# Stick-breaking attention: the mask as a product on TensorE instead of an operation on GpSimd and one on VectorE

## The chip, the cores and the metric

The kernel runs on one NeuronCore of a Trainium2 chip. The metric is the device time of one execution in microseconds (us), lower is better; where several runs are given it is their median. TensorE multiplies matrices into eight PSUM banks, VectorE, ScalarE and GpSimd work element by element, and SyncE issues the transfers of the weights.

## The reference, cut to what matters

The whole program is two stacked blocks of two layers each. The change is in the first block, in both of its layers: 256 tokens, 1024 columns, three attention branches beside each other, gates, an output projection and a feed-forward part. One of the three branches is stick-breaking attention, with 8 heads of 64 columns:

```python
z = jnp.einsum('bqhd,bkhd->bhqk', q_blk, k).astype(jnp.float32) * scale
past = kpos[None, :] < qpos[:, None]
log_beta = jax.nn.log_sigmoid(z)
log_one_minus = jnp.where(past, jax.nn.log_sigmoid(-z), 0.0)
remain = lax.cumsum(log_one_minus, axis=3, reverse=True) - log_one_minus
w = jnp.where(past, jnp.exp(log_beta + remain), 0.0)
return jnp.einsum('bhqk,bkhd->bqhd', w.astype(v.dtype), v)
```

A key counts only where it stands strictly before the query (`past`). The second block holds other mixers and a mixture of experts; it is the longer part of the time and isn't touched.

## The kernel before, in words

All large products are made in three parts: each float32 operand is split into a high part in float32r and a low remainder, and `three` (lines 324 to 330) multiplies high by high, low by high and high by low. Weights come in chunks of 128 x 2048 into a ring of six. For each chunk ScalarE makes the high part (`split`, line 530), VectorE the remainder (`split`, line 642), and TensorE frees the slot. Each engine runs one list of instructions in the order of the code; between engines semaphores count. A PSUM bank is taken with a wait on `free` (`Tensor.bank`) and freed by whoever reads it last.

The program is written by hand in stages, and the stage of the change is `stick_beside_inputs`. There are four routines that carry it, one for each engine, and in all of them stick-breaking attention is woven into the products that make the inputs of the next two branches (jobs QA0, QA1, KVA, QC0, QC1, KC0, KC1, and the values VC).

TensorE (lines 1010 to 1060) goes: logits of heads 0 to 3 into banks 0 to 3; the products of QA0, QA1 and KVA; the sums of heads 0 to 3; QC0; a transposition of values; output of heads 0 and 1; logits of heads 4 and 5; QC1; output of heads 2 and 3; logits of heads 6 and 7; KC0 and KC1; the sums of heads 4 to 7; the first half of VC; output of heads 4 and 5; the second half of VC; output of heads 6 and 7. Logits are keys by queries in three blocks of 128 columns: keys 0 to 127 by all 256 queries (line 1018) and keys 128 to 255 by the later queries (line 1019). Blocks 0 and 2 are the diagonal ones, in which the mask matters. A head has 64 columns, and two heads share a tile of 128 partitions: an even head lies in partitions 0 to 63, an odd one in 64 to 127, so the logits of a head use half of the array's rows.

For a head the chain is: logits; ScalarE takes the magnitude, Exp and Ln in place (lines 1213, 1218, 1223); VectorE adds the positive part (line 1428), which gives the softplus of the logits; GpSimd multiplies the diagonal blocks by 0 or 1 (`stick_heads`, line 843); TensorE adds the sums over later keys to the logits in the bank, by three float32 products (`sums`, lines 1026 to 1028); VectorE adds 0 or -1e30 to the result and writes it to SBUF, and frees the bank (`log_weights`, line 1434); ScalarE takes Exp (line 1228); TensorE multiplies by the values (`weigh_pair`, lines 477 and 478).

VectorE has, beside that and the splits, the turning of queries and keys by position (`turned_by_positions`, lines 712 to 717), called `rope` in the routine: one operation that reads the job's bank, four that read it by quarters of the partitions (line 714, the last of which frees the bank) and one addition. The bank of KC0 is 7, that of QC1 is 6, and VC takes banks 6 and 7.

In the second block, `decays_in` (lines 1778 to 1787) puts two products of 4 rows (256 and 128 columns) and two products of the identity with a mask of 128 columns, in float32, into one bank per head; `latent_heads` (line 1727) has products of 64 rows behind ordinary ones; `key_rows` (lines 1834 and 1835) has products of two heads in both halves of the rows.

Of the kernel before, what the change touches and what calls it, by code (L numbers as in the profile page):

```python
# [24 lines left out]
F32R = mybir.dt.float32r  # L25
# [108 lines left out]
def table_columns(parts):  # L134
# [8 lines left out]
A_TABLES, A_COLS = table_columns(SHARED_TABLES + [  # L143
    ("band", S), ("causal", S), ("before01", 3 * P), ("before", 3 * P), ("tri", P), ("ones", P)])
B_TABLES, B_COLS = table_columns(SHARED_TABLES + [
# [15 lines left out]
class Memory:  # L161


    def __init__(self, nc, ctx):
# [3 lines left out]
        def sem(name):  # L168
            return ctx.enter_context(nc.semaphore(name))
# [20 lines left out]
        self.unit_rows = nc.dram_tensor("unit_rows", (UNITS * P, D), F32, kind="Internal").ap()  # L190
        self.zeros = sb("zeros", [P, P], F32R)
        self.bank = [ctx.enter_context(nc.psum_tensor(f"bank{i}", [P, 512], F32))[:] for i in range(8)]

# [9 lines left out]
        self.x_loaded = sem("x_loaded")  # L203
        self.tables_loaded = sem("tables_loaded")
        self.cols_loaded = sem("cols_loaded")
        self.shared_loaded = sem("shared_loaded")
# [63 lines left out]
        self.n_ready = sem("n_ready")  # L270
        self.lom_ready = sem("lom_ready")
        self.logw_ready = sem("logw_ready")
        self.gate_in = sem("gate_in")
# [522 lines left out]
class Pool(Engine):  # L796
# [40 lines left out]

    def stick_heads(self, before):
        m = self.m
        for h in range(8):  # L840
            a = m.probs[:, h % 4, :].rearrange("p (n c) -> p n c", n=3)[:, 0:3:2, :]
            self.eng.wait_ge(m.n_ready, self.w.next(m.n_ready))
            self.isa.tensor_tensor(a, a, before, ALU.mult).then_inc(m.lom_ready, 1)


# [30 lines left out]
class TensorA(Tensor):  # L876
    def layer(self, layer):
# [9 lines left out]
        for job in STICK_IN[2:]:  # L887
            self.inputs(job)
        self.eng.wait_ge(m.qk_ready, w.next(m.qk_ready, 4))
        self.stick_beside_inputs()  # L890

# [118 lines left out]
    def stick_beside_inputs(self):  # L1010
# [4 lines left out]
        def logits(h):  # L1015
            q, k = (a_tile(m, x + h // 2)[(h % 2) * DH:(h % 2 + 1) * DH, :] for x in (QB, KB))
            bank = self.bank(h % 4)
            self.isa.matmul(bank[:, 0:S], k[:, 0:P], q, start=True, stop=False, skip_group_check=True)
            self.isa.matmul(bank[:, S:S + P], k[:, P:S], q[:, P:S], start=False, stop=False,
                            skip_group_check=True).then_inc(m.to_act[h % 4], 1)  # L1020

        def sums(h):
            bank, lom = m.bank[h % 4], m.probs[:, h % 4, :]
            tri, ones = m.tab(A_TABLES, "tri"), m.tab(A_TABLES, "ones")
            self.eng.wait_ge(m.lom_ready, self.w.next(m.lom_ready))
            self.isa.matmul(bank[:, 0:S], tri, lom[:, 0:S], start=False, stop=False, skip_group_check=True)
            self.isa.matmul(bank[:, P:S], ones, lom[:, S:S + P], start=False, stop=False, skip_group_check=True)
            self.isa.matmul(bank[:, S:S + P], tri, lom[:, S:S + P], start=False, stop=True,
                            skip_group_check=True).then_inc(m.to_dve[h % 4], 1)

# [25 lines left out]
        for half in range(2):  # L1056
            self.used(self.rows(banks, self.chunk(), 512, (m.hT_hi, m.hT_lo), 4, 4 * half, KT))
            if half == 0:
                out(4)
        out(6, 3)  # L1060

# [81 lines left out]
class ScalarA(Scalar):  # L1143
# [62 lines left out]
    def stick_beside_inputs(self, tile0):  # L1206
# [18 lines left out]
        def weights(h):  # L1225
            self.eng.wait_ge(m.logw_ready, self.w.next(m.logw_ready))
            self.eng.wait_ge(m.weighed, self.w.reuse(m.weighed))
            self.isa.activation(m.probsT[:, h % 2, :], m.probs[:, h % 4, :], ACT.Exp).then_inc(m.pt_ready, 1)

# [28 lines left out]
        for h in range(4, 8):  # L1258
            weights(h)
        self.oT_high(5, tile0, (4, 3))  # L1260
        self.inputs_out(VC)
        self.oT_high(7, tile0, (4, 3))

# [57 lines left out]
class VectorA(Vector):  # L1321
# [90 lines left out]
    def stick_beside_inputs(self, tile0, cos, sin):  # L1412
        m = self.m
        neg = m.tab(A_TABLES, "before")

# [14 lines left out]

        def log_weights():
            for hh in range(4):
                self.eng.wait_ge(m.to_dve[hh], self.w.next(m.to_dve[hh]))
                self.isa.tensor_tensor(m.probs[:, hh, :], m.bank[hh][:, 0:384], neg, ALU.add) \
                    .then_inc(m.logw_ready, 1)
                self.eng.drain().then_inc(m.free[hh], 1)

        self.settle()
# [5 lines left out]
        self.split(1)  # L1444
        log_weights()
        rope(QA1)
# [8 lines left out]
        magnitudes()  # L1455
        self.split(1)
        rope(KC0)
        self.split(1)
        log_weights()
        self.split(1)  # L1460
        rope(KC1)
        self.oT_low(2, tile0, (4, 3))
        self.oT_low(3, tile0, (4, 3))

# [1398 lines left out]
def program(nc, inp, out):  # L2863
    with ExitStack() as ctx:
# [52 lines left out]
        def _(pool):  # L2917
# [10 lines left out]
            for layer in range(DEPTH):  # L2928
                e.power((2, 4), 4)
                e.stick_heads(m.tab(A_TABLES, "before01").rearrange("p (n c) -> p n c", n=3)[:, 0:3:2, :])  # L2930

# [115 lines left out]
def tables_a():  # L3047
# [8 lines left out]
        band=np.concatenate([window, causal], 1), causal=np.concatenate([0 * one, causal], 1),  # L3056
        before01=np.concatenate([before, one, before], 1),
        before=np.concatenate([np.where(before, 0.0, NEG), 0 * one, np.where(before, 0.0, NEG)], 1),
        tri=np.where(i[:, None] >= i[None, :], -1.0, 0.0), ones=-one)
# [184 lines left out]
```

## Time and profile before

| | |
|---|---|
| median of 3 runs | 2347.61 us (2345.21 to 2348.76) |
| span of the profiled execution, first to last instruction | 2343.6 us |
| what lies around the span, if the span is that of the median run | 4.0 us |
| TensorE busy | 2297.0 us (98%) |
| VectorE busy | 1882.2 us (80%) |
| ScalarE busy | 1404.5 us (60%) |
| GpSimd busy | 69.3 us (3%) |

The profile is of one execution and gives its span; its device time is not listed apart from the three runs. Names in it: PE is TensorE, PEld its loading of weights, DVE VectorE, ACT ScalarE, POOL GpSimd, SP SyncE. A line such as L1018 is a line of the kernel before; a helper's line stands for all its callers. Products overlap in the pipeline, so the duration of one says less than the distance from one start to the next; the text reads starts. A float32 product leaves two records, one of float32r a single one; the type at the end of a row of TensorE is that of the bank. The stick-breaking stage of layer 0 lies at about 50 to 118 us, that of layer 1 at about 491 to 559 us.

### The profile page before, as it was taken

The page shows a single profiled execution, that of the slowest core. Times are in us where ns is not written, and L with a number is a line of the kernel's source. Part 1 is how long each engine was busy: PE and PEld are TensorE (multiplying, and loading weights), DVE is VectorE, ACT ScalarE, POOL GpSimd, SP SyncE. Part 2 cuts the span into 40 slices and gives each one's busy share as a digit, 9 for nine tenths or more (in the row PEclk, how much of TensorE's full clock was granted, in tenths as well). Part 3 has the DMA queues.
Part 4 walks back from the last instruction along what each step waited for, and adds up shares of the span by engine and source line. Part 5 has one row for each costly group of instructions (what it writes and reads, how often), then busy time and mean ns, then how long its engine had stood idle before and what let it go on. Part 6 is the DMA issues. An engine that isn't in the chain of part 4 may idle for free.

```text
span 2343.6 us, 34973 instructions
## 1 busy us (share of the span) xinstructions
PE 2297.0 (98%) x12998; PEld 1975.8 (84%) x12998; DVE 1882.2 (80%) x2158; ACT 1404.5 (60%) x1396; POOL 69.3 (3%) x81
## 2 busy tenths in 40 slices
PE   9999999999999999989999989999999999999997
PEld 8877999997789998779989778888888888888886
DVE  5977898768779987774457879888988898989897
ACT  5565544455654435634336547777777777777764
POOL 0100000000000000000000010000000000000000
PEclk9999999999999999999999999999999999999999
DMA  6444555444365556268544359999999999999995
GB/s 257 144 162 177 209 190 180 175 168 153 137 219 195 195 181 213 98 224 263 195 179 162 138 230 392 379 376 380 387 376 382 376 385 374 386 374 387 374 398 211
DMA packets 93418, 608.15 MB, mean 259 GB/s; under 512 B 9696, under 2 KB 18032, under 8 KB 22656
## 3 DMA queue, kind: packets, MB, share of 16 engines
q1 hardware_dynamic: 88064, 584.69, 66.3%
q0 software_dynamic: 5248, 22.02, 2.4%
q8 instruction: 70, 1.15, 0.2%
q14 instruction: 36, 0.29, 0.0%
HBM read 591.47 MB, written 15.20 MB: 259 GB/s over the span
## 4 chain that ended last, share of the span: by engine, by line
PE 85%; DVE 8%; DVEq 2%; ACT 2%; issue 1%; DMA 1%; POOL 1%; ACTq 0%; POOLq 0%; SPq 0%
PE bank L328 27%; PE bank L330 26%; PE bank L329 26%; DVEq L634 2%; DVE w_lo L642 2%; DMA raw<-in_weights_dram 1%; PE bank L1978 1%; DVE nat L714 1%; DVE probs L729 1%; PE bank L437 0%; PE bank L447 0%; PE bank L400 0%; PE bank L380 0%; PE bank L477 0%; ACT w_hi L530 0%
## 5 line engine op out<-in xcount | busy, mean ns | idle before, releaser
L642 DVE TENSOR_TENSOR w_lo<-raw,w_hi 128x2048 fp32r<-128x2048 f32 x547 | 1239.1, 2289 | 253.2 <-ACT w_hi L530 230.5
L530 ACT CAST w_hi<-raw 128x2048 fp32r<-128x2048 f32 x547 | 1037.3, 1913 | 223.0 <-DMA raw<-in_weights_dram 215.4
L328 PE MATMUL bank<-w_hi,hT_hi 128*128 128x512 f32 (+1 forms) x1248 | 496.5, 398 | 7.6 <-DVEq L2726 2.6
L330 PE MATMUL bank<-w_hi,hT_lo 128*128 128x512 f32 (+1 forms) x1248 | 486.5, 390 | 0.0
L329 PE MATMUL bank<-w_lo,hT_hi 128*128 128x512 f32 (+1 forms) x1248 | 485.5, 389 | 0.0
L328 PE MATMUL bank<-hT_hi,w_hi 128*128 128x256 f32 x1552 | 443.6, 286 | 2.5 <-DVEq L663 1.7
L330 PE MATMUL bank<-hT_hi,w_lo 128*128 128x256 f32 x1552 | 440.3, 284 | 0.0
L329 PE MATMUL bank<-hT_lo,w_hi 128*128 128x256 f32 x1552 | 440.2, 284 | 0.0
L328 PE MATMUL bank<-w_hi,oT_hi 128*128 128x512 f32 x940 | 370.6, 394 | 1.5 <-DVE oT_lo L2739 1.2
L329 PE MATMUL bank<-w_lo,oT_hi 128*128 128x512 f32 x940 | 366.4, 390 | 0.0
L330 PE MATMUL bank<-w_hi,oT_lo 128*128 128x512 f32 x940 | 366.2, 390 | 0.0
L328 PEld LDWEIGHTS bank<-hT_hi,w_hi 128*128 128x128 f32 x1552 | 298.0, 192 | 6.9 <-issue 4.7
L329 PEld LDWEIGHTS bank<-hT_lo,w_hi 128*128 128x128 f32 x1552 | 298.0, 192 | 1.7 <-issue 0.5
L330 PEld LDWEIGHTS bank<-hT_hi,w_lo 128*128 128x128 f32 x1552 | 297.9, 192 | 0.0
L328 PEld LDWEIGHTS bank<-w_hi,hT_hi 128*128 128x128 f32 x1248 | 235.5, 189 | 60.1 <-issue 13.8
L330 PEld LDWEIGHTS bank<-w_hi,hT_lo 128*128 128x128 f32 x1248 | 235.1, 188 | 49.1
L329 PEld LDWEIGHTS bank<-w_lo,hT_hi 128*128 128x128 f32 x1248 | 235.7, 189 | 44.4
L328 PEld LDWEIGHTS bank<-w_hi,oT_hi 128*128 128x128 f32 x940 | 176.6, 188 | 40.0 <-issue 3.7
L330 PEld LDWEIGHTS bank<-w_hi,oT_lo 128*128 128x128 f32 x940 | 176.4, 188 | 37.5
L329 PEld LDWEIGHTS bank<-w_lo,oT_hi 128*128 128x128 f32 x940 | 176.8, 188 | 34.1
L1549 DVE SCALAR_TENSOR_TENSOR probs<-probs,all_cols 128x254 f32<-128x254 f32 (+1 forms) x176 | 77.3, 480 | 6.9 <-issue 0.4
L1295 ACT ACTIVATE probs<-probs 128x512 f32<-128x512 f32 x22 | 13.9, 633 | 107.0 <-DVE probs L1549 107.0
(314 smaller groups left out, 1586.6 us busy)
## 6 DMA issues: line engine op xcount, KB each, us to landing
raw<-in_weights_dram SPq DMA_DIRECT2D x547, 1024.0 KB, 4.9
token_rows<-all_cols SPq DMA_DIRECT2D x11, 512.0 KB, 9.4
arena<-in_norms_dram POOLq DMA_DIRECT2D x4, 1024.0 KB, 9.2
nat<-token_rows POOLq DMA_DIRECT2D x7, 512.0 KB, 8.1
unit_rows<-probs POOLq DMA_DIRECT2D x7, 512.0 KB, 6.9
arena<-in_b_gate_dram POOLq DMA_DIRECT2D x6, 512.0 KB, 4.1
unit_rows<-all_cols SPq DMA_DIRECT2D x5, 512.0 KB, 9.6
tables<-in_tables_b_dram POOLq DMA_DIRECT2D x1, 1216.0 KB, 5.7
```

The lines of the kernel that those rows point to most:

```text
L328: mm(out, st[0], mv[0], start=start, stop=False, skip_group_check=True)
L329: mm(out, st[0], mv[1], start=False, stop=False, skip_group_check=True)
L330: return mm(out, st[1], mv[0], start=False, stop=stop, skip_group_check=True)
L530: self.isa.copy(m.w_hi[:, slot, :], m.raw[:, slot, :]).then_inc(m.hi_ready, 1)
L634: self.eng.drain()
L642: self.isa.tensor_tensor(m.w_lo[:, slot, :], m.raw[:, slot, :], m.w_hi[:, slot, :].bitcast(F32), ALU.subtract).then_inc(m.lo_ready, 1)
L714: last = self.isa.tensor_tensor(tmp[to:to + 32], src[a:a + 32], s[a:a + 32], ALU.mult)
L729: last = self.isa.tensor_tensor_reduce(m.probs[:, hh, a:e], m.bank[b][:, a:e], mk, self.scale, first(h), ALU.add, ALU.max, m.small[:, 16 + ...
L1295: self.isa.activation(g, g, ACT.Silu).then_inc(m.silu_done, 1)
L1549: last = self.isa.scalar_tensor_tensor(out, bank[:, g * S:(g + 1) * S - back], col(g, 2 - back), out, ALU.mult, ALU.add)
L1978: last = self.isa.transpose(bank[:, k * P:(k + 1) * P], h_rows(m)[:, k * P:(k + 1) * P], m.tab(B_TABLES, "ident"))
```

## The change

GpSimd's mask and VectorE's additions are taken out (with the semaphores `lom_ready` and `logw_ready`), and the two mask tables of 384 columns become one of 128, `hidden`, with 0 or -2^100. A new tile `exact` holds the identity and `hidden` in float32r; GpSimd copies them there once, in layer 0, and TensorE waits for that (`exact_ready`) ahead of the first logits. Behind the two products of every head's logits TensorE gets a third, of the full array: the identity by `hidden`, repeated over blocks 0 and 2, added in the bank. With it the softplus of a hidden logit is zero without a mask, and so is the Exp of its sum. The sums now wait for VectorE's `n_ready` and signal ScalarE, which takes Exp straight from the bank and frees the bank. VectorE's turning of KC0 moves ahead of a split. The output of heads 6 and 7 goes to bank 2 in place of bank 3.

```diff
         def logits(h):
             q, k = (a_tile(m, x + h // 2)[(h % 2) * DH:(h % 2 + 1) * DH, :] for x in (QB, KB))
             bank = self.bank(h % 4)
             self.isa.matmul(bank[:, 0:S], k[:, 0:P], q, start=True, stop=False, skip_group_check=True)
-            self.isa.matmul(bank[:, S:S + P], k[:, P:S], q[:, P:S], start=False, stop=False,
+            self.isa.matmul(bank[:, S:S + P], k[:, P:S], q[:, P:S], start=False, stop=False, skip_group_check=True)
+            later = bank[:, 0:384].rearrange("p (n c) -> p n c", n=3)[:, 0:3:2, :]
+            ident, hidden = m.exact[:, 0:P], m.exact[:, P:2 * P]
+            self.isa.matmul(later, ident, hidden.unsqueeze(1).to_broadcast([P, 2, P]), start=False, stop=False,
                             skip_group_check=True).then_inc(m.to_act[h % 4], 1)
...
         def sums(h):
...
-            self.eng.wait_ge(m.lom_ready, self.w.next(m.lom_ready))
+            self.eng.wait_ge(m.n_ready, self.w.next(m.n_ready))
...
-                            skip_group_check=True).then_inc(m.to_dve[h % 4], 1)
+                            skip_group_check=True).then_inc(m.to_act[h % 4], 1)
...
         def weights(h):
-            self.eng.wait_ge(m.logw_ready, self.w.next(m.logw_ready))
+            self.eng.wait_ge(m.to_act[h % 4], self.w.next(m.to_act[h % 4]))
             self.eng.wait_ge(m.weighed, self.w.reuse(m.weighed))
-            self.isa.activation(m.probsT[:, h % 2, :], m.probs[:, h % 4, :], ACT.Exp).then_inc(m.pt_ready, 1)
+            self.isa.activation(m.probsT[:, h % 2, :], m.bank[h % 4][:, 0:384], ACT.Exp).then_inc(m.pt_ready, 1)
+            self.eng.drain().then_inc(m.free[h % 4], 1)
...
@@ VectorE, stick_beside_inputs
         magnitudes()
         rope(QA0)
         self.split(1)
-        log_weights()
         rope(QA1)
...
         rope(QC1)
         magnitudes()
-        self.split(1)
         rope(KC0)
-        self.split(1)
-        log_weights()
-        self.split(1)
+        self.split(3)
         rope(KC1)
-        self.oT_low(2, tile0, (4, 3))
-        self.oT_low(3, tile0, (4, 3))
+        self.oT_low(2, tile0, (4, 2))
+        self.oT_low(3, tile0, (4, 2))
...
@@ GpSimd, for each layer
                 e.power((2, 4), 4)
-                e.stick_heads(m.tab(A_TABLES, "before01").rearrange("p (n c) -> p n c", n=3)[:, 0:3:2, :])
+                if layer == 0:
+                    pool.wait_ge(m.shared_loaded, 16)
+                    nc.gpsimd.tensor_copy(m.exact[:, 0:P], m.tab(A_TABLES, "ident"))
+                    pool.wait_ge(m.tables_loaded, 16)
+                    nc.gpsimd.tensor_copy(m.exact[:, P:2 * P], m.tab(A_TABLES, "hidden"))
+                    pool.drain().then_inc(m.exact_ready, 1)
```

## Rows read from the trace of the kernel before

**Rows 1.** Page, parts 1 and 4: busy us (share) xinstructions; the chain's shares by engine

```profile
PE 2297.0 (98%) x12998; PEld 1975.8 (84%) x12998; DVE 1882.2 (80%) x2158; ACT 1404.5 (60%) x1396; POOL 69.3 (3%) x81
...
PE 85%; DVE 8%; DVEq 2%; ACT 2%; issue 1%; DMA 1%; POOL 1%; ACTq 0%; POOLq 0%; SPq 0%
```

**Rows 2.** Timeline of TensorE, later sums: start, us, operation, [idle before <- releaser]

```profile
99.90 0.60 PE L1026 MATMUL bank<-probs,tables 128*128 128x256 f32 x2
...
102.12 0.70 PE L1026 MATMUL bank<-probs,tables 128*128 128x256 f32 x2 [0.30 <-POOL probs L843]
...
105.17 0.47 PE L328 MATMUL bank<-w_hi,hT_hi 128*128 128x512 f32 x1 [1.03 <-issue]
...
542.93 0.70 PE L1026 MATMUL bank<-probs,tables 128*128 128x256 f32 x2 [0.68 <-POOL probs L843]
...
545.98 0.47 PE L328 MATMUL bank<-w_hi,hT_hi 128*128 128x512 f32 x1 [1.03 <-issue]
```

**Rows 3.** Timeline of VectorE, layer 0, beside the later sums

```profile
97.26 1.95 DVE L1428 SCALAR_TENSOR_TENSOR probs<-bank,probs 128x384 f32<-128x384 f32 x4
99.13 2.36 DVE L642 TENSOR_TENSOR w_lo<-raw,w_hi 128x2048 fp32r<-128x2048 f32 x1
...
102.28 2.79 DVE L714 TENSOR_TENSOR nat<-bank,tables 32x512 f32<-32x512 f32 x4
```

**Rows 4.** Line 843: operation xcount, ns min/median/max, first and last start

```profile
L843 POOL TENSOR_TENSOR probs<-probs,tables x16: 721/742/2772, 62.3 to 542.8; 128x256 f32<-128x256 f32 x16
```

**Rows 5.** Timelines of GpSimd, ScalarE and TensorE, layer 0, single rows

```profile
22.07 0.72 POOL L835 TENSOR_TENSOR small<-small 128x2 f32<-128x2 f32 x1 [12.36 <-DVE small L682]
...
81.97 0.95 ACT L1228 ACTIVATE probsT<-probs 128x384 f32<-128x384 f32 x2
...
87.43 0.71 PE L1018 MATMUL bank<-arena 64*128 64x256 f32 x4
```

**Rows 6.** Timeline of TensorE, layer 0, logits of heads 0 to 3

```profile
50.44 0.71 PE L1018 MATMUL bank<-arena 64*128 64x256 f32 x4
50.98 0.40 PE L1019 MATMUL bank<-arena 64*128 64x128 f32 x4
...
52.05 0.39 PE L328 MATMUL bank<-hT_hi,w_hi 128*128 128x256 f32 x1
52.27 0.28 PE L329 MATMUL bank<-hT_lo,w_hi 128*128 128x256 f32 x1
52.39 0.29 PE L330 MATMUL bank<-hT_hi,w_lo 128*128 128x256 f32 x1
```

**Rows 7.** Timeline of TensorE, layer 0, logits of heads 4 and 5

```profile
79.81 0.71 PE L1018 MATMUL bank<-arena 64*128 64x256 f32 x4
...
80.67 0.39 PE L328 MATMUL bank<-hT_hi,w_hi 128*128 128x256 f32 x1
80.90 0.28 PE L329 MATMUL bank<-hT_lo,w_hi 128*128 128x256 f32 x1
```

**Rows 8.** Timeline of TensorE, second block, `decays_in`: one head, then the next

```profile
988.88 0.69 PE L1782 MATMUL bank<-nat,tables 4*128 4x256 f32 x2
...
989.73 0.71 PE L1785 MATMUL bank<-tables 128*128 128x128 f32 x4
990.37 0.69 PE L1782 MATMUL bank<-nat,tables 4*128 4x256 f32 x2
```

**Rows 9.** Timeline of TensorE, second block, from an ordinary product to 64 rows

```profile
943.31 0.28 PE L330 MATMUL bank<-hT_hi,w_lo 128*128 128x256 f32 x1
943.52 0.91 PE L1727 MATMUL bank<-arena 64*128 64x128 f32 x8
```

**Rows 10.** Timeline of TensorE, second block, pairs of heads around full-array products

```profile
973.78 0.55 PE L447 MATMUL bank<-tables,probs 128*128 128x128 f32 x3
974.25 0.71 PE L1834 MATMUL bank<-arena 64*128 64x256 f32 x4
```

**Rows 11.** Who waited for whom, TensorE, whole span: us, times, longest

```profile
PE bank L447 <- DVE probs L763: 3.4, 4, 1.2
```

More of the change, by code:

```diff
@@ L143 @@
 A_TABLES, A_COLS = table_columns(SHARED_TABLES + [
-    ("band", S), ("causal", S), ("before01", 3 * P), ("before", 3 * P), ("tri", P), ("ones", P)])
+    ("band", S), ("causal", S), ("hidden", P), ("tri", P), ("ones", P)])
 B_TABLES, B_COLS = table_columns(SHARED_TABLES + [
@@ L191, in __init__ @@
         self.zeros = sb("zeros", [P, P], F32R)
+        self.exact = sb("exact", [P, 2 * P], F32R)
         self.bank = [ctx.enter_context(nc.psum_tensor(f"bank{i}", [P, 512], F32))[:] for i in range(8)]
@@ L204, in __init__ @@
         self.tables_loaded = sem("tables_loaded")
+        self.exact_ready = sem("exact_ready")
         self.cols_loaded = sem("cols_loaded")
@@ L270, in __init__ @@
         self.n_ready = sem("n_ready")
-        self.lom_ready = sem("lom_ready")
-        self.logw_ready = sem("logw_ready")
         self.gate_in = sem("gate_in")
@@ L836, in power @@
             .then_inc(m.rstd, 1)
[L838 to L843, printed above, removed]
 STICK_IN = [
@@ L889, in layer @@
         self.eng.wait_ge(m.qk_ready, w.next(m.qk_ready, 4))
+        if layer == 0:
+            self.eng.wait_ge(m.exact_ready, w.next(m.exact_ready))
         self.stick_beside_inputs()
@@ L1059, in stick_beside_inputs @@
                 out(4)
-        out(6, 3)
+        out(6, 2)
     def turn_values(self):
@@ L1259, in stick_beside_inputs @@
             weights(h)
-        self.oT_high(5, tile0, (4, 3))
+        self.oT_high(5, tile0, (4, 2))
         self.inputs_out(VC)
-        self.oT_high(7, tile0, (4, 3))
+        self.oT_high(7, tile0, (4, 2))
     def softmax_beside(self, tile0, sinks=False):
@@ L1413, in stick_beside_inputs @@
         m = self.m
-        neg = m.tab(A_TABLES, "before")
         def rope(job):
@@ L1429, in magnitudes @@
                     .then_inc(m.n_ready, 1)
[L1431 to L1436, printed above, removed]
         self.settle()
@@ L2929, in _ @@
                 e.power((2, 4), 4)
-                e.stick_heads(m.tab(A_TABLES, "before01").rearrange("p (n c) -> p n c", n=3)[:, 0:3:2, :])
+                if layer == 0:
+                    pool.wait_ge(m.shared_loaded, 16)
[3 more added lines that the diff above has]
+                    pool.drain().then_inc(m.exact_ready, 1)
                 for i in (1, 0, 2):
@@ L3056, in tables_a @@
         band=np.concatenate([window, causal], 1), causal=np.concatenate([0 * one, causal], 1),
-        before01=np.concatenate([before, one, before], 1),
-        before=np.concatenate([np.where(before, 0.0, NEG), 0 * one, np.where(before, 0.0, NEG)], 1),
+        hidden=np.where(before, 0.0, -2.0 ** 100),
         tri=np.where(i[:, None] >= i[None, :], -1.0, 0.0), ones=-one)
```

## The prediction

> **What bounds the kernel now.** I read the shares of the engines and the chain that ended last first: TensorE is busy for 98% of the span, and 85% of the chain lies on it [rows 1]. So an edit counts by what it does to TensorE: a wait that it takes away, or work that it puts into TensorE's queue. Work taken from VectorE, ScalarE or GpSimd is worth only the TensorE wait that it ends. The second view is the list of TensorE's idle stretches. In the stick-breaking stage there are two in each layer: one before the sums of a later head, released by GpSimd's mask (line 843), 0.30 us in layer 0 and 0.68 us in layer 1, and one of 1.03 us before the first product of the values VC in either layer [rows 2]. The profile calls the second "issue". Its real releaser is found by time: the products go into banks 6 and 7, bank 7 holds KC0 until the fourth line-714 operation of that job's turning has read it, and these four start at 102.28 and take 2.79 us, so they end at 105.07; TensorE starts at 105.17 [rows 2, 3]. All that TensorE can get back in the two stages is 0.30 + 0.68 + 1.03 + 1.03 = 3.04 us. Elsewhere in them it goes from one instruction to the next, so each instruction added is paid in full.
>
> **What goes, and what it is worth.** GpSimd's 16 masks (median 742 ns, longest 2.77 us) go [rows 4], and with them VectorE's 16 additions (line 1434). For TensorE the first is worth the 0.98 us of its waits: the sums now wait for VectorE's maximum (line 1428), and the four of the second quartet are done at 97.26 + 1.95 = 99.2, before TensorE came to the first of those sums at 99.90 [rows 2, 3]. TensorE will arrive later than that, by what is added below, so the wait doesn't come back. The additions stand before ScalarE's Exp, and the products that need the Exp came later without a wait, so their going is worth nothing. Nor is GpSimd's freedom.
>
> The turning of KC0 moves ahead of one split, the one at 99.13 that took 2.36 us [rows 3]. It is six VectorE instructions and no DMA, and it will release bank 7 at about 102.7 in place of 105.07. Sums without GpSimd's wait would end at 103.8 and, with TensorE delayed, later, so both waits of 1.03 us go. The split behind it belongs to the gate unit that follows the stage, more than 10 us later; it is hidden by the VC products, and would cost at most the 4.2 us of the turning if that cover were gone. What is late next is no engine beside TensorE but TensorE's own queue.
>
> **What is only shifted.** GpSimd gets two copies of 128 x 128 in layer 0, behind its power instruction at 22.07 and a wait for tables; TensorE's first logits come at 50.44 [rows 5, 6], over 25 us later, and behind the wait GpSimd has nothing until the weighed products. The new wait of TensorE therefore costs nothing. The load of the tables, 640 columns narrower, is waited for by nobody on TensorE in that stretch. ScalarE now reads Exp's input from the bank and frees the bank; the pair of Exps at 81.97 takes 0.95 us and banks 2 and 3 are wanted again at 87.43 [rows 5], a cover of 4.5 us. Behind these Exps on ScalarE stands a cast for a chunk that is used later still. If the cover were gone, TensorE would wait for the difference, at every reuse of those banks. The last output moves from bank 3 to bank 2, which ScalarE has emptied two Exps earlier; nothing.
>
> **What is added on TensorE.** Each of 16 heads gets a product of the full array (128 rows) behind its logits, which use 64 rows: an even head the upper half, an odd head the lower. Three things happen.
>
> *The heads lose their company.* A head has two products, each of which leaves two records. Yet the trace shows four records of line 1018 in a row and then line 1019 four times, from 50.44 on [rows 6]: two heads run side by side in the two halves. A pair takes 79.81 to 80.67, 0.86 us [rows 7]. What one head takes alone is shown in a later stage, where a routine puts the same column counts through 4 rows with no partner: 988.88 to 989.73, 0.85 us [rows 8]. So a single head costs what a pair costs. With a full-array product between the even and the odd head, I take it that the odd head can't start before it is done.
>
> *The product itself.* It has 256 columns in the one-record float32r form. Such a product takes 0.12 us in a stream (52.27 to 52.39) but 0.22 when it comes first after a 64-row product (52.05 to 52.27; 80.67 to 80.90 gives 0.23) [rows 6, 7].
>
> *The way back.* From a 256-column float32r product to one of 64 rows it is 0.21 us (943.31 to 943.52) in place of 0.12, 0.09 more [rows 9]. The mask routine of [rows 8] agrees: 989.73 to 990.37 is 0.64 us for four passes of 128 columns, which at 0.11 each would be 0.44, so 0.20 for going to the full array and back; mine are 0.10 + 0.09.
>
> A head then costs 0.85 + 0.22 + 0.09 = 1.16 us, and a group of n heads n x 1.16 less the last 0.09, since ordinary products of the full array follow. Before, the group of two cost 80.90 - 79.81 - 0.12 = 0.97, the group of four 52.27 - 50.44 - 0.12 = 1.71. Groups of two get 2.23 - 0.97 = 1.26 us longer, the group of four 4.55 - 1.71 = 2.84. A layer has one group of four and two of two: 5.36 us; both layers 10.7 us. The nearest rows bound it: with 0.21 us from mask to next head and no surcharge, a head is 1.06, and the sum falls by 1.6 to 9.1; with 0.20 us for either change in place of 0.10, 1.27 a head, and it rises by 1.8 to 12.5. I take 10.7, since the mask routine of rows 8, the same pattern, gives its 0.20 for the two.
>
> The Trainium skill, "TensorEngine Tiling (Array Packing)", Key Properties, says that changing the tiling mode drains TensorE; it speaks against this change, which raises the changes from one pair in a group to one in a head. The trace agrees with 0.10 and 0.09 us a change. Were changes free, the sum would be lower by about 16 x 0.19 = 3.0 us.
>
> **The sum.** 10.7 - 3.0 = +7.7 us. Against the profiled execution's span of 2343.6 that is 2351.3; what lies around the span is 4.0 us if the span belongs to the median run, so against the median of 2347.6 I say 2355.3, 0.33% slower. About 0.2%, 4.7 us, is what a measurement of this kernel can tell from no change.
>
> **The rivals.**
> *First, not slower: the pairs stay together.* TensorE lets the odd head run past the even head's mask, as it lets it run past the even head's second product [rows 6]. Its place is each pair's first mask. A pair then costs 0.86 + 0.22 + 0.12 + 0.09 = 1.29, groups of two 1.20 (+0.23), the group of four 2.49 (+0.78): 1.24 a layer, 2.5 in all, and the net is 2.5 - 3.0 = -0.5: 2347.1. About 1.0 us hangs on each of the eight pairs: three that stay together bring the change within 0.2%, all eight are needed for no loss. Against it: after a full-array product at 973.78 the next pair waits until 974.25, when the third of them is through [rows 10], though that row has both halves behind the product.
> *Second: the heads were serial already.* If the records of rows 6 mislead and no two heads ever ran side by side, the groups of before would be 1.60 and 2.90 us (four heads at 0.65 and 0.30 for the changes), the changes would add 0.63 and 1.65, 5.8 in all, and the time would be 2350.4. Against it stand the 0.86 us for two heads beside 0.85 for one [rows 7, 8]. The Trainium skill, "TensorE: Matmul & The Clock Gate", Part 3 (The mechanism), says that matmuls start strictly in program order; by that rule this rival would be the case and the net +2.8, but the four line-1018 records in a row differ from it, and the measurement decides.
>
> *Third: the relief runs on.* VectorE enters the first softmax earlier and ends the four waits of 3.4 us on its division (line 763) [rows 11]. Then +4.3: 2351.9. Against: VectorE's entry is gated by ScalarE's copy of the last output, which follows the VC products and moves with TensorE.
>
> *Fourth: the stage's waits stay.* If ScalarE or VectorE is late in a new place, for instance bank 7 still the last, the 2.06 us of the moved turning are not won: 2357.4.
>
> **How the numbers follow.** Forecast (serial heads) 0.80; first rival 0.09, second 0.03, third 0.04, fourth 0.04. The forecast's own range is 9.1 - 3.0 to 12.5 - 3.0, that is 2353.7 to 2357.1, and about 1.3 us either way for the runs' own spread. The range for all must leave out at most 2 in 10: it goes down to the second rival, 2350, and up to 2358.5; the first stays outside. Slower by over 0.2% (above 2352.3) holds the forecast but for a little and the fourth rival: 0.82. Within 0.2%: the first, second and third: 0.15. Faster by over 0.2% needs 4.7 us, more than all 3.0 us of waits: 0.03.
>
> **What would show it.** In the changed profile: no TensorE wait before line 1026's successor and none before VC's first product (else the fourth rival). Logits of one head alone: two records of the first product, two of the second, then one mask, 1.1 to 1.2 us from head to head; if four records of one line still stand in a row, the first rival. From the first logits to the ordinary products 4.5 us in place of 1.6 in the group of four, 2.2 in place of 0.86 in the groups of two. The first softmax should keep its waits on line 763's successor. The forecast is wrong if a head's distance is below 0.8 us, or if a wait on ScalarE or VectorE over 1 us stands in the stage.

## The result and the profile after

The changed kernel takes 2354.55 us (median of five runs, 2352.64 to 2356.20); the kernel before takes 2345.74 us (median of five, the three shown ahead of the prediction among them). The ratio, made from the means of the runs, is 1.0033 with a 95% interval of 1.0022 to 1.0044: the change makes the kernel 0.33% slower. The profiled execution took 2354.55 us with a span of 2352.9 us, against a span of 2343.6 before.

The page of the changed kernel, engines (busy us, share, instructions) and the shares of the chain that ended last:

```profile
PE 2308.9 (98%) x13014; PEld 1984.6 (84%) x13014; DVE 1873.3 (80%) x2142; ACT 1405.1 (60%) x1396; POOL 54.4 (2%) x67
...
PE 88%; DVE 6%; DVEq 2%; DMA 1%; issue 1%; ACT 1%; POOL 0%; POOLq 0%; SPq 0%
```

TensorE has the 16 added products and is 11.9 us busier; VectorE and GpSimd, which were not the bound, lost 8.9 and 14.9 us [rows 1]. The work moved from engines with room to the one without.

What [rows 6] and [rows 7] showed of before looks like this in the timeline of TensorE in the changed kernel, layer 1 (start, us, operation, records):

```profile
494.82 0.70 PE L1013 MATMUL bank<-arena 64*128 64x256 f32 x2
495.36 0.38 PE L1014 MATMUL bank<-arena 64*128 64x128 f32 x2
495.67 0.38 PE L1017 MATMUL bank<-exact 128*128 128x256 f32 x1
495.98 0.70 PE L1013 MATMUL bank<-arena 64*128 64x256 f32 x2
...
499.15 0.38 PE L1017 MATMUL bank<-exact 128*128 128x256 f32 x1
499.37 0.28 PE L328 MATMUL bank<-hT_hi,w_hi 128*128 128x256 f32 x1
```

Each line now has two records in a row in place of four: a head runs alone, then its mask. From head to head it is 495.98 - 494.82 = 1.16 us, and the group of four takes 499.37 - 494.82 = 4.55 us. Both are the forecast's figures to the hundredth. A group of two takes 2.23 us (83.02 to 85.25 in layer 0), which is the forecast's figure too.

For the rest of this text the stage is measured in one way: from the first record of the logits of heads 0 to 3 to the first product of the branch that follows the stage (the scores, line 437). TensorE does the same ordinary products in between in all kernels, so a difference of these distances is what an edit costs in the stage. The rows at which it begins and ends, TensorE, before (layer 0, end; its start is in [rows 6]) and after (layer 0, start and end; layer 1, end):

```profile
118.11 0.93 PE L437 MATMUL bank<-arena 64*128 64x128 f32 x8
...
49.30 0.70 PE L1013 MATMUL bank<-arena 64*128 64x256 f32 x2
...
122.05 0.93 PE L437 MATMUL bank<-arena 64*128 64x128 f32 x8
...
566.07 0.93 PE L437 MATMUL bank<-arena 64*128 64x128 f32 x8
```

It is the measure to use here: in two traces of the changed kernel it repeats to 0.01 us, while the runs of one kernel lie several us apart, partly because the stretch behind the second stage, which no edit touches, took between 1784.65 and 1789.78 us in the traces of this case.

| distance in us | layer 0 | layer 1 | both |
|---|---|---|---|
| before | 67.67 | 68.07 | 135.74 |
| after | 72.75 | 71.25 | 144.00 |
| difference | +5.08 | +3.18 | +8.26 |

The span grew by 9.3 us. Of that 8.26 lies in the two stages, -1.14 in the opening ahead of the first logits (which took 49.30 to 51.81 us in the traces of this case, and 49.37 in one with the same opening as before), 0.0 between the stages, and +2.2 behind the second one, in code that is the same in both kernels; both differences are inside what these stretches vary by and are not put down to the change.

The 1.50 us by which layer 0 exceeds layer 1 was not forecast. It is a clock. Windows of the changed kernel in layer 0 (us, busy time and instructions of PE, PEld, DVE, ACT and POOL, then PEclk, the share of the DMA engines, GB/s):

```profile
48.00:53.00 5.00, 5.00 (x23) 3.57 (x22) 0.00 (x0) 2.47 (x5) 0.00 (x0) 1.00 0.48 170
53.00:57.00 4.00, 4.00 (x19) 3.68 (x19) 0.16 (x1) 2.76 (x4) 0.00 (x0) 0.57 0.16 66
57.00:61.00 4.00, 4.00 (x36) 4.00 (x35) 2.65 (x2) 3.94 (x6) 0.00 (x0) 1.00 0.02 4
```

The granted clock of the middle window is 0.57: TensorE ran at 1.2 GHz for most of it and at 2.4 GHz on both sides. The timeline of TensorE in the changed kernel shows the same in single products, from the last of the four heads of layer 0 on:

```profile
53.35 0.63 PE L1014 MATMUL bank<-arena 64*128 64x128 f32 x2
53.92 0.58 PE L1017 MATMUL bank<-exact 128*128 128x256 f32 x1
54.30 0.41 PE L328 MATMUL bank<-hT_hi,w_hi 128*128 128x256 f32 x1
54.51 0.41 PE L329 MATMUL bank<-hT_lo,w_hi 128*128 128x256 f32 x1
...
56.64 0.30 PE L330 MATMUL bank<-hT_hi,w_lo 128*128 128x256 f32 x1
```

The last head's second product takes 0.63 us where the one of layer 1 takes 0.38, and ordinary products start 0.21 us apart in place of 0.12 until 56.64. In layer 1 the same instructions show a granted clock of 1.00 and 0.12 us. More on the clock stands below.

In the list of TensorE's idle stretches, none lies in either stage any more. The wait behind the stage on the division of the first softmax stands where it stood, as in [rows 11]:

```profile
PE bank L447 <- DVE probs L763: 3.4, 4, 1.2
```

### The profile page after: what moved, and what is told of

Its sections match the earlier page's. It is cut to its first block, busy times and chain, and to the rows that moved or that the text cites. A ratio compares the mean times of both kernels' runs of the same rounds, so it can differ in the third digit from the quotient of the medians.

```text
span 2352.9 us, 34976 instructions
## 1 busy us (share of the span) xinstructions
PE 2308.9 (98%) x13014; PEld 1984.6 (84%) x13014; DVE 1873.3 (80%) x2142; ACT 1405.1 (60%) x1396; POOL 54.4 (2%) x67
## 4 chain that ended last, share of the span: by engine, by line
PE 88%; DVE 6%; DVEq 2%; DMA 1%; issue 1%; ACT 1%; POOL 0%; POOLq 0%; SPq 0%
PE bank L328 27%; PE bank L330 27%; PE bank L329 27%; DMA raw<-in_weights_dram 1%; DVE w_lo L642 1%; DVEq L634 1%; PE bank L1965 1%; DVE probs L729 1%; PE bank L477 1%; PE bank L437 0%; PE bank L1013 0%; PE bank L447 0%; PE bank L400 0%; PE bank L1714 0%; DVE probs L763 0%
```

## The experiments

Two theories stood against each other at the start. *First:* the masks cost what they cost by their place, because a full-array product between two heads ends the overlap of the heads and adds two changes of tile shape; grouped behind all heads they would be nearly free. *Second:* the product is dear in itself. Beside them two questions were open: what the waits that went were worth, and which part of the change ended them. Every ratio below is to the kernel before, run again beside the kernel of the experiment (its medians lay between 2345.47 and 2346.20 us), with its 95% interval. A kernel that ran once has no ratio; there only the distances in its trace count.

### The masks behind all heads of a group

```diff
-        def logits(h):
+        def logits(*heads):
+            for h in heads: products(h)
+            for h in heads: mask(h)
...
-            logits(0); logits(1); logits(2); logits(3)
+            logits(0, 1, 2, 3)
```

and likewise `logits(4, 5)` and `logits(6, 7)`.

> The changed kernel with the order of a group turned: all its heads' logits first, then all its masks (groups of four, two and two). Nothing is left out. Theory 1 (the mask between two heads costs their company and two changes of the array's shape each): the heads of a pair run side by side again, four records of the first logits' line in a row; a mask costs 0.12 us and the way to the full array is paid once a group, as before. The group of four takes 0.5 us more than in the kernel before, each group of two 0.24, together 1.9 us in both layers; the waits that are gone are worth 4.0 us by the distances in the changed trace, so the time is about 2.1 us below the kernel before and 8 to 10.5 below the changed one. Theory 2 (the masks cost what they cost in any place, 10.7 / 16 = 0.67 us each): no gain on the changed kernel. Theory 3 (a drop of the granted clock after the first group makes a good part of the loss): a gain of about 1.5 us on the changed kernel if the drop goes, and the groups as long as there.

Median 2344.70 us against 2345.47 before, ratio 0.9997 (0.9988 to 1.0006). Both stages 66.80 us (50.11 to 116.91 in layer 0). Timeline of TensorE in this kernel, layer 0:

```profile
50.11 0.71 PE L1019 MATMUL bank<-arena 64*128 64x256 f32 x4
...
50.86 0.70 PE L1019 MATMUL bank<-arena 64*128 64x256 f32 x4
...
51.72 0.73 PE L1026 MATMUL bank<-exact 128*128 128x256 f32 x4
52.29 0.28 PE L328 MATMUL bank<-hT_hi,w_hi 128*128 128x256 f32 x1
...
116.91 0.93 PE L437 MATMUL bank<-arena 64*128 64x128 f32 x8
```

The four records of a line in a row are back, and the four masks run as one stream. The stages are 10.4 us below those of the changed kernel (144.00 - 133.60, of which 1.5 is the clock), and 2.1 below before. The runs say the same of the changed kernel: 0.9997 here and 1.0033 there, with intervals that do not meet. The same 16 products cost 10.76 us in one order and 1.86 in the other (the next experiment gives the level without them), so the first theory holds. Against the kernel before, the 2 us can't be told from no change by the runs.

### No mask on TensorE at all

```diff
-            self.isa.matmul(later, ident, hidden.unsqueeze(1).to_broadcast([P, 2, P]), ...).then_inc(m.to_act[h % 4], 1)
```

with the signal put on the second product.

> The changed kernel without the mask product: the hidden keys are left unmasked; all else, waits and turning too, as changed. This gives the worth of the waits that are gone, apart from what is added. If the forecast's 3.0 us (the sum of the idle stretches) is their worth, 3.0 us below the kernel before; if each wait also costs the products around it a restart, as the distances in the changed trace say (1.8 us in layer 0, 2.2 in layer 1), 4.0 us below. Theory 1: the groups of logits as long as before (1.61 us to the first ordinary product in the group of four, 0.86 in those of two), no drop of the clock. If some wait had come back in a new place, it stands in this trace too.

Median 2343.34 us, ratio 0.9991 (0.9982 to 1.0001). Both stages 65.87 us. TensorE, layer 0, no mask, start and end of the stage:

```profile
49.67 0.71 PE L1013 MATMUL bank<-arena 64*128 64x256 f32 x4
...
115.54 0.93 PE L437 MATMUL bank<-arena 64*128 64x128 f32 x8
```

This kernel leaves the hidden keys unmasked. It gives the two terms of the forecast's sum apart. The masks between the heads cost 71.25 - 65.87 = 5.38 us a layer at the full clock, 10.76 in both; grouped, they cost 66.80 - 65.87 = 0.93 a layer, 0.12 each. What went from the kernel before without any addition on TensorE is 1.80 us in layer 0 and 2.20 in layer 1, 4.00 in all, where the forecast had 3.04.

### The turning moved, and nothing else (on the kernel before)

```diff
         magnitudes()
-        self.split(1)
         rope(KC0)
-        self.split(1)
+        self.split(2)
         log_weights()
```

> The kernel before with one edit: VectorE's turning of KC0 ahead of the split; GpSimd's masks and VectorE's additions stay. The wait before the first VC product goes in both layers if bank 7 was its releaser: 2.06 us by the idle stretches, about 2.5 with the restart; the waits on GpSimd (0.3 and 0.7 us) stay or grow a little. 2.0 to 2.5 us below the kernel before. If the releaser was another (the chunk, bank 6), the wait stays and so does the time.

Median 2344.32 us, ratio 0.9998 (0.9988 to 1.0007). The stages take 66.71 and 67.08 us, about 1.0 less than before in each. The wait before VC is gone, and so are the waits on GpSimd's masks: the four masks of the later heads took 4.86 us in the kernel before, where VectorE's split ran beside the third of them, and 2.83 here, where the turning did. GpSimd, kernel before:

```profile
97.90 4.86 POOL L843 TENSOR_TENSOR probs<-probs,tables 128x256 f32<-128x256 f32 x4 [32.79 <-DVE probs L1428]
```

GpSimd, turning moved alone:

```profile
96.82 2.83 POOL L843 TENSOR_TENSOR probs<-probs,tables 128x256 f32<-128x256 f32 x4 [32.78 <-DVE probs L1428]
```

Yet the stages stay 0.84 and 1.21 us above those without a mask. In their place a new wait has come, at the output of heads 4 and 5. TensorE, layer 1, turning moved alone:

```profile
547.95 0.65 PE L477 MATMUL bank<-probsT,arena 128*64 128x256 f32 x2 [0.50 <-ACT probsT L1228]
...
548.65 0.65 PE L477 MATMUL bank<-probsT,arena 128*64 128x256 f32 x2
...
549.44 0.50 PE L328 MATMUL bank<-w_hi,hT_hi 128*128 128x512 f32 x1
```

ScalarE at that place, turning moved alone:

```profile
547.38 0.52 ACT L1228 ACTIVATE probsT<-probs 128x384 f32<-128x384 f32 x1 [5.79 <-DVE probs L1434]
```

VectorE there, turning moved alone:

```profile
546.78 2.64 DVE L1434 TENSOR_TENSOR probs<-bank,tables 128x384 f32<-128x384 f32 x4
```

TensorE waits 0.50 us (0.11 in layer 0) for an Exp that waits for VectorE's additions, and since the two Exps come one after the other, the two outputs do too: two records of a line in a row. They take 549.44 - 547.95 = 1.49 us, where a pair side by side takes 0.80 (a pair of the kernel before starts at 79.01, and what follows it at 79.81 [rows 7]). So 0.69 us of the 1.21 is lost company and the rest about the wait. No run takes the additions alone away; but by this chain of output, Exp and additions, taking them from VectorE, which the forecast held to be worth nothing, is worth this 0.84 and 1.21 us as soon as the other waits are gone.

### The mask product twice

```diff
             self.isa.matmul(later, ident, hidden..., start=False, stop=False, skip_group_check=True)
+            self.isa.matmul(later, ident, hidden..., start=False, stop=False, skip_group_check=True).then_inc(...)
```

> The changed kernel with every mask product issued twice, one behind the other (-2^101 in place of -2^100, the result is the same). Theory 1: the second is a full-array product behind a full-array product, so it costs about 0.12 us, 16 of them 1.9 us above the changed kernel, 1.28 us from head to head in place of 1.16. Theory 2 (the product itself is dear): 16 x 0.31 to 0.67, 5 to 10.7 us above it. Theory 3: the drop of the clock comes no more often, or comes in layer 1 too and adds some 1.5 us.

Median 2356.05 us, ratio 1.0047 (1.0032 to 1.0062). Both stages 72.20 us. TensorE, layer 0, mask doubled:

```profile
49.78 0.70 PE L1013 MATMUL bank<-arena 64*128 64x256 f32 x2
...
50.62 0.39 PE L1017 MATMUL bank<-exact 128*128 128x256 f32 x1
50.85 0.28 PE L1019 MATMUL bank<-exact 128*128 128x256 f32 x1
51.06 0.70 PE L1013 MATMUL bank<-arena 64*128 64x256 f32 x2
```

A head takes 1.28 us in place of 1.16: the second mask costs 0.12 each, 0.95 a layer (72.20 - 71.25). The product is cheap, and the second theory falls. Layer 0 is not longer than layer 1 here: the clock did not drop.

### Two heads of the same half beside each other

On the kernel with the masks grouped:

```diff
-            logits(0, 1, 2, 3)
+            logits(0, 2, 1, 3)
```

> The kernel with the masks behind their group, but the first group's logits in the order of heads 0, 2, 1, 3: heads 0 and 2 lie in the same half of the rows. No mask stands between them and the shape of the array doesn't change, so this is the loss of company alone. Theory 1 (a head runs beside the one behind it in the queue if that lies in the other half): 0 alone, 2 beside 1, 3 alone, three turns of 0.65 us in place of two: from the first logits to the first sums 0.65 us more than with masks last (20.1 us in place of 19.44), in both layers. Rival (TensorE looks further ahead and finds head 1 past head 2): 19.44, no change. Rival (no head has company; the 1.16 us are all changes of shape): no change.

One run: 2349.14 us; both stages 67.46, 0.66 above the grouped kernel. TensorE, layer 0:

```profile
50.21 0.70 PE L1019 MATMUL bank<-arena 64*128 64x256 f32 x2
...
50.96 0.70 PE L1019 MATMUL bank<-arena 64*128 64x256 f32 x4
...
51.73 0.59 PE L1019 MATMUL bank<-arena 64*128 64x256 f32 x2
...
52.47 0.74 PE L1026 MATMUL bank<-exact 128*128 128x256 f32 x4
```

Head 0 runs alone, heads 2 and 1 side by side, head 3 alone: three steps in place of two, no change of tile shape added. TensorE did not bring head 1 past head 2 to run beside head 0. The loss of one pair's company is 0.66 us. The rest of this run's time lies in the stretch behind the second stage (1789.6 us), where nothing was edited.

### Masks behind each pair

On the kernel with the masks grouped:

```diff
-            logits(0, 1, 2, 3)
+            logits(0, 1)
+            logits(2, 3)
```

> The kernel with the masks behind their group, but the first group of four cut in two pairs, each followed by its two masks: the pairs keep their company and there is one more way to the full array and back. This is the price of the changes of shape alone. Theory 1: 0.10 + 0.09 us for these, and what the two pairs lose by no longer overlapping at their seam: 0.2 to 0.35 us from first logits to first sums above masks last (19.65 to 19.8 us in place of 19.44). If the change of shape is what is dear and company nothing (0.4 us and more a change), 20.2 and above.

One run: 2347.72 us; both stages 67.14. TensorE, layer 0:

```profile
49.30 0.71 PE L1019 MATMUL bank<-arena 64*128 64x256 f32 x4
...
50.16 0.50 PE L1026 MATMUL bank<-exact 128*128 128x256 f32 x2
50.59 0.71 PE L1019 MATMUL bank<-arena 64*128 64x256 f32 x4
...
51.80 0.28 PE L328 MATMUL bank<-hT_hi,w_hi 128*128 128x256 f32 x1
```

All pairs stay together; the one further way into the full array and back costs 0.33 us. That holds whatever the two pairs lose by no longer overlapping at their seam, which no run takes apart from the change of shape. With this the 5.38 us a layer come apart: eight masks at 0.12 (0.93), four lost companies at 0.66 (2.64), and five more ways into the full array and back than without masks (eight in place of three) at 0.33 (1.65), 5.2 in all. The 0.33 was measured between two pairs and is carried over to the places inside a pair; 0.16 us a layer is left unexplained.

### The turning put back, in the changed kernel

```diff
         magnitudes()
+        self.split(1)
         rope(KC0)
-        self.split(3)
+        self.split(2)
         rope(KC1)
```

> The changed kernel with VectorE's turning of KC0 put back behind the split; masks stay between the heads. In the changed trace bank 7 is free at 106.2 us and the sums end at 109.2: a slack of 3.0 us, more than the 2.3 us of the split, since the masks delay TensorE. If that is right, the moved turning is worth nothing there: no wait before the VC products, the stage as long as in the changed kernel (71.25 us without a drop of the clock), the time the same. If the move is what ended the wait (the forecast's 2.06 us), the 1.03 us come back in each layer. It is also another look at the clock behind the first group: a drop of the granted clock there adds 1.5 us to that layer.

Median 2353.93 us, ratio 1.0034 (1.0020 to 1.0048), as the changed kernel; layer 1 takes 71.24 us against 71.25. VectorE of this kernel, layer 0:

```profile
108.06 2.79 DVE L714 TENSOR_TENSOR nat<-bank,tables 32x512 f32<-32x512 f32 x4
```

TensorE of this kernel, layer 0:

```profile
111.54 0.48 PE L328 MATMUL bank<-w_hi,hT_hi 128*128 128x512 f32 x1
```

Bank 7 is free at 108.06 + 2.79 = 110.85 and TensorE comes to VC at 111.54, without a wait. Layer 1, in which the clock did not fall, has the same 0.69 us between them (554.85 and 555.54). TensorE's delay by the masks had already ended the wait: in the changed kernel the moved turning is worth nothing.

### The turning put back, with the masks grouped

The same edit on the grouped kernel.

> The same put back in the kernel with the masks behind their group, in which TensorE comes earlier: bank 7 is free at 102.3 us and the sums end at 103.9, a slack of 1.7 us, less than the split's 2.3. So here a wait of some 0.6 us should come back in each layer: 67.4 to 67.6 us from the first logits to the next branch's scores in place of 66.80, 1.2 to 1.6 us in all. If the slack of the turning had nothing to do with the masks, 0 or 2.06 us.

Median 2346.03 us, ratio 1.0001 (0.9991 to 1.0010); 0.63 us more a layer (67.43 against 66.80). TensorE, layer 0:

```profile
103.32 0.39 PE L1035 MATMUL bank<-probs,tables 128*128 128x128 f32 x2
104.09 0.47 PE L328 MATMUL bank<-w_hi,hT_hi 128*128 128x512 f32 x1 [0.39 <-issue]
```

VectorE of that kernel:

```profile
101.21 2.79 DVE L714 TENSOR_TENSOR nat<-bank,tables 32x512 f32<-32x512 f32 x4
```

Bank 7 is free at 104.00, TensorE starts at 104.09. Where TensorE isn't late by itself, the moved turning is worth 0.63 us a layer. This run also shows how a listed idle is to be read. In the changed kernel, without a wait, the same two products stand 0.14 us apart:

```profile
108.93 0.39 PE L1026 MATMUL bank<-probs,tables 128*128 128x128 f32 x2
109.07 0.47 PE L328 MATMUL bank<-w_hi,hT_hi 128*128 128x512 f32 x1
```

Here it is 104.09 - 103.32 = 0.77, so 0.63 is lost, while the list says 0.39: it counts from the end of the record (0.39 us long), but the next product would have started 0.14 us after that record's start. At these two products a wait is worth the listed idle plus 0.25 us. At others it is another figure: at the outputs of heads 4 and 5, with the turning moved alone, the listed 0.50 us of layer 1 cost 0.57 by the starts (547.07 to 547.95 is 0.89; without a mask and without a wait the same two stand 0.32 apart, 107.90 to 108.22).

### Masks ahead of the products

On the grouped kernel:

```diff
         def logits(*heads):
-            for h in heads: products(h)
             for h in heads: mask(h)
+            for h in heads: products(h)
```

The mask opens the bank (`start=True`), the second product signals.

> Each group's masks ahead of its logits in place of behind them; nothing is left out. Theory 1: the masks then stand in the stream of ordinary products (or behind the outputs), 0.12 us each, and the array changes its shape as often as before: 0.45 to 0.5 us for the group of four and 0.23 to 0.25 for a group of two, 66.8 us a stage as with masks last, about 2.1 us below the kernel before by the traces. If the order inside a group matters (ScalarE gets all heads of a group at its end, TensorE changes from the outputs' shape to the full array and on to 64 rows in the groups of two), up to 0.2 us more for each group of two: 67.2.

Median 2347.37 us, ratio 1.0002 (0.9993 to 1.0012). TensorE, layer 0, the group of heads 4 and 5:

```profile
80.00 0.40 PE L478 MATMUL bank<-probsT,arena 128*64 128x128 f32 x4
80.33 0.50 PE L1027 MATMUL bank<-exact 128*128 128x256 f32 x2
80.76 0.71 PE L1019 MATMUL bank<-arena 64*128 64x256 f32 x4
```

From the ordinary product ahead of the first group to the scores a layer takes 67.52 us, against 67.12 with the masks behind: 0.40 more. (The count starts at that product because the change to 64 rows lies inside the first group here, and just ahead of its first record in the other kernel.) The groups of two stand behind an output of 128*64, so masks ahead of them add one more change of shape in each, about 0.2 us (the group of heads 4 and 5 with its output takes 0.18 more, the group of four 0.01); masks behind them need none, since ordinary products of the full array follow.

### The changed kernel once more

No edit; a second trace, for the clock.

> The changed kernel as it is, another look. In its first trace the granted clock was half for 3.4 us right behind the four heads of layer 0, and that layer's first group was 1.5 us longer than layer 1's; with the turning put back it was so again; with two masks a head it was not. If the drop belongs to the pattern of serial heads, it stands behind layer 0's or layer 1's group in this look too (23.3 us from first logits to first sums there, 21.82 without); if it was chance, both layers show 21.82. All other distances of the stage as in the first look, to 0.05 us.

One run: 2354.29 us; stages 72.74 and 71.24 us. The half clock of layer 0 is there again, with the same 1.50 us.

## Why the prediction was right

The forecast was 2355.3 us with 1.0033 to the time before, and 2354.55 with 1.0033 was measured. Its direction and its main term stand; two smaller terms were off, by -0.96 and +1.50 us, and partly cancel.

**What bounds.** Right: TensorE's added work was paid in full, and the work taken from VectorE and GpSimd gave back no more than TensorE's own waits.

**What is added.** Forecast 10.7 us, measured 2 x 5.38 = 10.76. A head costs what the forecast's sum has for it: heads run alone (two records in a row), 0.85 us from a head's start to its mask (494.82 to 495.67) and 0.31 from the mask to the next head (495.67 to 495.98), which is its 0.22 + 0.09. What these figures are made of was split otherwise: two heads of 0.85 for a pair of 0.86 put 0.84 on a lost pairing, and a way into the full array and back got 0.10 + 0.09; the runs have 0.66 and 0.33. The mask itself stands, at 0.12. The estimate from the mask routine of a later stage [rows 8] carried over to this one. The Trainium skill, "TensorEngine Tiling (Array Packing)", Key Properties, says that a change of the tiling mode drains TensorE; the runs agree, with 0.33 us for one way there and back in the group of four. The largest part here, 2.64 of 5.38 us a layer, is that a full-array product between two heads ends their overlap.

The prediction's remark that free changes would lower the sum by 16 x 0.19 = 3.0 us counts too many of them: groups ended in the full array before too, so by the prediction's own terms the change adds five ways a layer, and 10 x 0.19 = 1.9.

**What goes.** The term that was off is that of 3.04 us: 4.00 were won. The four stretches were taken as listed, 0.30, 0.68, 1.03 and 1.03 us [rows 2]. Each is worth about 0.25 more. The run with the turning put back showed that for the wait before VC; carried over to the two waits on GpSimd it fits both layers: 0.55 + 1.28 = 1.83 for layer 0 (measured 1.80) and 0.93 + 1.28 = 2.21 for layer 1 (2.20).

Two attributions inside that term were wrong as well. The forecast gave 2 x 1.03 to the moved turning; in the changed kernel it is worth nothing, since the masks make TensorE late enough (turning put back: 71.24 against 71.25). And it held the going of VectorE's additions to be worth nothing; with the turning moved alone they hold up the outputs of heads 4 and 5, by the trace, and the stages are 0.84 and 1.21 us longer than without a mask. The sentence "the products that need the Exp came later without a wait" was true of the kernel before, in which TensorE was held elsewhere; it was not asked again with those waits gone.

**What was not in the sum.** The half clock in layer 0, +1.50 us. So the stages add up to 10.76 + 1.50 - 4.00 = +8.26 us where the forecast had +7.7.

**What is only shifted.** Right: no wait in either stage on GpSimd's copies, ScalarE's freeing of the banks, or bank 2.

**The base.** The forecast took 4.0 us around the span from a median of three runs. More runs of the same kernel have their median at 2345.74, 2.1 us around it, and the changed kernel's profiled execution has 1.6. A sum 1.6 us too small for the span and 2.4 us too much around it leave the forecast only 0.75 us above the measured time, so that this closeness is partly luck; the ratio is the better comparison, and its interval is 2.6 us wide to either side.

**The rivals.** *First* (the pairs stay together): refuted by two records in a row and 1.16 us from head to head; the run with masks behind each pair shows what keeps a pair together, namely that nothing of the full array stands between its heads. *Second* (serial already): refuted by the run with two heads of the same half side by side, where losing company costs 0.66 us. The Trainium skill, "TensorE: Matmul & The Clock Gate", Part 3 (The mechanism), says that matmuls keep program order in start and end; the four records of one line in a row, which are two heads at the same time, differ from it in every kernel that has the pairs. *Third* (the relief runs on): refuted, the waits on the softmax are still 3.4 us. *Fourth* (the stage's waits stay): refuted, no idle stretch is left in the stage. Its mechanism, a new place of lateness, appeared with the turning moved alone.

## What to carry to other kernels

When small products share the array side by side, put full-array products behind the whole group and not between its members: eight masks cost 5.38 us a layer between the heads and 0.93 behind them, by nothing but their order. Work that moves from idle engines to the engine that bounds is paid in full, and what it relieves is worth only the bound engine's waits; ask about each relief again with the other waits gone. Measure a wait on TensorE by the distance of starts against the same pair of instructions without it, not by the listed idle time.

## What the runs showed of the hardware that was not expected

TensorE's clock fell to 1.2 GHz with no gap in TensorE's work. In layer 0 of the changed kernel the clock is 1.00 while the first three heads run one behind the other; from about 53.3 us, in the fourth head, to 56.7 us it is the lower one, and ordinary products start 0.21 us apart in place of 0.12; the granted clock of 53 to 57 us is 0.57, where the kernel before has 1.00 there. It cost 1.47 to 1.50 us, in all three traces of kernels with one mask behind each head (the changed kernel, the same once more, and the one with the turning put back), always in layer 0 and never in layer 1. It did not occur with the mask doubled, nor where heads run in pairs. The four serial heads are therefore not enough to bring it about; what else does is open. Falls elsewhere can have a gap ahead of them: in the kernel before, TensorE was busy for only 1.20 us of 895 to 899 us, and the granted clock of 899 to 902 us is 0.50.

One of GpSimd's four masks is what made the 4.86 us. In the kernel before, the third mask of the later heads starts 0.17 us after VectorE's split of 2.36 us [rows 3], and it takes 2.77 us:

```profile
99.30 2.77 POOL L843 TENSOR_TENSOR probs<-probs,tables 128x256 f32<-128x256 f32 x1
```

It ends 0.58 us after the split does. Layer 1 has the same, with 2.77 us. The mask ahead of it, which was already running when the split began, took 0.74. That one and the other thirteen of that kernel took 0.72 to 0.76 us, those beside VectorE's maxima (line 1428) and its turning among them, and with the turning moved alone, where no split runs beside a mask, all sixteen took 0.73 to 0.76. So it is the split that holds a mask up; its two inputs lie in SBUF, while the maxima and the first operation of the turning read a bank. Whether that is why was not tested.
